# Gates, projections and merge computed with tokens on partitions in a two-layer decoder trunk

## What is computed

```python
xn = rms_norm(x, norm_mix_g[l])
gates = sigmoid(xn @ w_gate[l] + b_gate[l]).reshape(B, S, 4, D)
merged = (gates[:, :, 0] * (ya @ w_proj_a[l]) + gates[:, :, 1] * (yb @ w_proj_b[l])
          + gates[:, :, 2] * (yc @ w_proj_c[l]) + gates[:, :, 3] * (yd @ w_proj_d[l]))
x = x + merged @ w_o[l]
hn = rms_norm(x, norm_ffn_g[l])
x = x + (silu(hn @ w_gate_half) * (hn @ w_up_half)) @ w_ffn_out[l]
```

## Time and profile before

| | us |
|---|---|
| median of 3 runs | 843.73 |
| lowest and highest run | 842.5 and 844.55 |
| the profiled execution, time | 843.07 |
| the profiled execution, span | 841.3 |

### The profile page before, as it was taken

The page is one execution under the profiler, slowest core; times in us unless marked ns, Lnnn a source line. Parts: engine busy times, 40 slices in busy tenths (PEclk is TensorE's granted clock), DMA queues, the critical chain, the costliest instruction groups (busy, mean ns, idle before and its releaser), DMA issues.

```text
span 841.3 us, 15196 instructions
## 1 busy us (share of the span) xinstructions
PE 826.8 (98%) x6199; PEld 783.6 (93%) x6199; DVE 615.8 (73%) x729; ACT 465.9 (55%) x658; POOL 161.1 (19%) x153
## 2 busy tenths in 40 slices
PE   7999999999999999999999999999999999999995
PEld 6999999999989999999999999999999999999995
DVE  5889987776786657665787999767678766566654
ACT  5856787625554555445464567855346454545452
POOL 2814764065000000000000474503300000000000
PEclk9999999999999999999999999999999999999998
DMA  8884544558464554645567464445545456554621
GB/s 261 265 258 138 187 151 154 174 176 237 150 200 145 207 199 155 226 168 200 157 214 230 151 201 152 150 151 165 190 150 198 153 197 207 192 184 165 215 112 50
DMA packets 122070, 152.15 MB, mean 181 GB/s; under 512 B 3824, under 2 KB 109634, under 8 KB 122016
## 3 DMA queue, kind: packets, MB, share of 16 engines
q1 hardware_dynamic: 119392, 148.39, 54.0%
q0 software_dynamic: 1328, 1.81, 0.9%
q10 hardware_dynamic: 1296, 1.20, 0.4%
HBM read 148.23 MB, written 1.05 MB: 177 GB/s over the span
## 4 chain that ended last, share of the span: by engine, by line
PE 93%; DVE 3%; ACT 2%; issue 1%; DMA 1%; ACTq 0%; DVEq 0%
PE bank L875 19%; PE bank L876 19%; PE bank L877 19%; PE bank L941 19%; PE bank L943 10%; PE bank L932 1%; PE bank L934 1%; PE bank L933 1%; DVE w_lo L1274 1%; ACT w_hi L589 1%; PE bank L1025 1%; DMA gain_rows<-in_norm_ffn_g 1%; DVE sq L1305 1%; PE bank L1046 1%; PE bank L921 0%
## 5 line engine op out<-in xcount | busy, mean ns | idle before, releaser
L1274 DVE TENSOR_TENSOR w_lo<-raw,w_hi 128x2048 fp32r<-128x2048 f32 x136 | 318.8, 2347 | 126.8 <-ACT w_hi L589 126.3
L589 ACT ACTIVATE w_hi<-raw 128x2048 fp32r<-128x2048 f32 (+1 forms) x144 | 264.1, 1839 | 146.1 <-PE bank L877 124.2
L941 PE MATMUL bank<-act,w_hi 128*128 128x512 f32 x704 | 246.6, 393 | 0.0
L875 PE MATMUL bank<-act,w_hi 128*128 128x256 f32 x768 | 220.0, 286 | 2.1 <-DVE w_lo L1568 1.0
L876 PE MATMUL bank<-act,w_hi 128*128 128x256 f32 x768 | 217.3, 283 | 0.0
L877 PE MATMUL bank<-act,w_lo 128*128 128x256 f32 x768 | 217.3, 283 | 0.0
L943 PE MATMUL bank<-act,w_lo 128*128 128x256 f32 x704 | 197.1, 280 | 0.0
L941 PEld LDWEIGHTS bank<-act,w_hi 128*128 128x128 f32 x704 | 131.8, 187 | 28.7
L875 PEld LDWEIGHTS bank<-act,w_hi 128*128 128x128 f32 x768 | 147.3, 192 | 4.6 <-issue 2.1
L876 PEld LDWEIGHTS bank<-act,w_hi 128*128 128x128 f32 x768 | 147.4, 192 | 0.1
L877 PEld LDWEIGHTS bank<-act,w_lo 128*128 128x128 f32 x768 | 147.3, 192 | 0.0
(11 more groups left out here) (219 smaller groups left out, 1032.4 us busy)
## 6 DMA issues: line engine op xcount, KB each, us to landing
raw<-in_w_ffn_in SPq DMA_DIRECT2D x44, 1024.0 KB, 5.1
raw<-in_w_gate SPq DMA_DIRECT2D x32, 1024.0 KB, 5.5
raw<-in_w_ffn_out SPq DMA_DIRECT2D x22, 1024.0 KB, 4.9
raw<-in_w_in SPq DMA_DIRECT2D x20, 1024.0 KB, 6.0
raw<-in_w_o SPq DMA_DIRECT2D x8, 1024.0 KB, 5.1
raw<-in_w_proj_b SPq DMA_DIRECT2D x4, 1024.0 KB, 4.9
gates<-qk SPq DMA_DIRECT2D x32, 64.0 KB, 4.7
raw<-in_w_proj_a SPq DMA_DIRECT2D x2, 1024.0 KB, 4.9
```

The lines of the kernel that those rows point to most:

```text
L589: return nc.scalar.activation(o, i, ACT.Copy)
L875: nc.tensor.matmul(o, whi, ahi, start=first, stop=False, skip_group_check=skip)
L941: nc.tensor.matmul(bank[b + f], hi[:, k, fs], act2[:, k, :, :].rearrange("p h s -> p (h s)"), start=(k == 0), stop=False, skip_group_check ...
L1274: V.tensor_tensor(w_lo[slot][:, :], raw[slot][:, :], w_hi[slot][:, :].bitcast(F32), ALU.subtract)\
```

## The change

The 16 gate units of a layer come in pairs. A pair covers 512 weight columns: its first unit holds the first half of the contraction, its second unit the other. Tokens are stationary, 512 weight columns move: 24 matmuls in a unit. A pair fills two banks, one for each half of the tokens. The projections use the same layout (`proj_rows`). The gates' bias now varies along the free axis, so it is loaded from HBM over all partitions (`load_bias`, seven loads in a layer), and DVE multiplies by 1/rms and adds the bias in one instruction (`gate_in`). The merged sum has tokens on partitions, so PE transposes it (`merged_turn`, 8 transposes after unit 30 and 8 after unit 32). The output projection takes its contraction in halves: units 32 and 33 use the first half for channels 0 to 511 and 512 to 1023, units 34 and 35 the second (`unit_wo`, still 48 matmuls 256 wide). Updates of x move accordingly.

```diff
+def pair_of(u):
+    branch, j = gate_of(u)
+    nth = (u - U_GATE) // 2 if u < U_PROJ_A else 6 + j // 2
+    return branch, j // 2, nth, [(u - j % 2 + t) % 4 for t in range(2)]
+BIAS_LOADS = {14: (0, 0), 15: (0, 1), 19: (2, 0), 21: (2, 1), 23: (1, 0), 25: (1, 1), 26: (3, 0)}
...
@@ sync @@
+            def load_bias(l, branch, h):
+                if branch == 3:
+                    buf, n = 2, 2 * 512
+                    sp.wait_ge(s_done, (l + 1) * 2 * HP)
+                else:
+                    buf, n = h, 512
+                    nth = GATE_BRANCH.index(branch)
+                    if nth:
+                        for u in (U_GATE + 4 * (nth - 1) + 2 * h, U_GATE + 4 * (nth - 1) + 2 * h + 1):
+                            sp.wait_ge(bank_free[u % 4], free_at(l, u % 4, f"unit{u}", True))
...
+                sp.dma_start(bias_bufs[buf][:, 0:n], T["b_gate"][l][c0:c0 + n].partition_broadcast(P))\
+                    .then_inc(bias_in[buf], 16)
...
@@ scalar @@
+                elif gate_of(u) and gate_of(u)[1] % 2 == 1:
+                    branch, h, _, bt = pair_of(u)
+                    for t in range(TT):
+                        act.wait_ge(bank_free[bt[t]], free_at(l, bt[t], f"unit{u - 1 + t}", True))
+                        k = branch * KT + 4 * h + 2 * t
+                        nc.scalar.activation(gates[:, k:k + 2, :], gates[:, k:k + 2, :], ACT.Tanh, scale=0.5)\
+                            .then_inc(gate_ready, 1)
+                elif u in (U_GATE_D + 2, U_WO):
+                    for i in (0, 1) if u < U_WO else (2, 3):
+                        act.wait_ge(mt_done, l * 4 + i + 1)
+                        copy(y_hi[:, 2 * i:2 * i + 2, :], low(4 + i)).then_inc(act_hi_ready, 1)
+                elif u in (U_WO + 2, U_WO + 3):
+                    for i in (0, 1) if u == U_WO + 2 else (2, 3):
+                        xg_hi(l, 1, i)
...
-                if U_WO <= u < U_FFN:
-                    square(l, 1, u - U_WO)
+                if u in (U_WO + 2, U_WO + 3):
+                    for i in (0, 1) if u == U_WO + 2 else (2, 3):
+                        square(l, 1, i)
...
-                    urgent = u in (U_WO - 1, U_FFN - 1)
+                    urgent = u > U_GATE_D
...
@@ tensor @@
+            def unit_tokens(slot, half, out_banks, tile=None):
...
+                    for k in range(4):
+                        kk = 4 * half + k
+                        nc.tensor.matmul(o, act_hi[:, kk, ts], hi[:, k, :], start=(kk == 0), stop=False)
+                        nc.tensor.matmul(o, act_hi[:, kk, ts], lo[:, k, :], start=False, stop=False)
+                        last = nc.tensor.matmul(o, act_lo[:, kk, ts], hi[:, k, :], start=False, stop=(kk == KT - 1))
...
+            def merged_turn(l, h):
+                pe.wait_ge(merged_ready, l * 4 + 2 * h + 2)
...
+                            last = nc.tensor.transpose(low(b)[:, f, t * P:(t + 1) * P],
+                                                       merged(2 * h + t)[:, (2 * j + f) * P:(2 * j + f + 1) * P],
+                                                       ident[:, :])
+                    last.then_inc(mt_done, 1)
...
+                    if u == U_GATE_D + 2:
+                        merged_turn(l, 0)
...
+                for j in range(4):
+                    u, (kh, c) = U_WO + j, divmod(j, 2)
                     weights(l, u % RING, u // RING)
...
+                    pe.wait_ge(act_lo_ready, l * 12 + (4 + 2 * kh + 2))
...
+                    unit_wo(u % RING, kh, c)
+                    if j == 0:
+                        merged_turn(l, 1)
...
-                    if i == 3:
-                        norm_stat(l, 1)
                     for f in range(2):
                         last = ffn_half(slot, 0, f, (2 * i, 2 * i + 1))
                         if f == 0 and i == 3:
                             last.then_inc(half_done, 1)
+                            norm_stat(l, 1)
...
@@ vector @@
+                V.scalar_tensor_tensor(gates[:, k:k + 2, :], low(bt[t]), rms_t[:, t:t + 1],
+                                       gate_bias(branch, h).rearrange("p (f s) -> p f s", f=2),
+                                       ALU.mult, ALU.add)\
+                    .then_inc(bank_free[bt[t]], 1)
...
+                if u in (U_GATE_D + 1, U_GATE_D + 3):
...
+                    for t in range(TT):
+                        gate_in(l, u, t)
+                        merge_d(l, 2 * h + t)
...
+                if u == U_WO + 2:
+                    dve.wait_ge(tile_done, l * 10 + 9)
+                    x_update(l, 1, 0)
                     unit_done(l, u)
...
+                    x_update(l, 1, 1)
+                    xg_lo(l, 1, 0)
+                    xg_lo(l, 1, 1)
+                if u == U_WO + 3:
+                    dve.wait_ge(tile_done, l * 10 + 10)
+                    x_update(l, 1, 2)
+                    square_sum(l, 1, 1)
+                    xg_lo(l, 1, 2)
+                    unit_done(l, u)
+                    x_update(l, 1, 3)
+                    square_sum(l, 1, 2)
+                    xg_lo(l, 1, 3)
+                    square_sum(l, 1, 3)
```

More of the change, by code:

```diff
@@ L188, in build @@
         par = sb("par", [P, N_ROWS])
-        half_bg = sb("half_bg", [P, 32])
         half_cn = sb("half_cn", [P, 4])
@@ L282, in build @@
         merged_ready = sem("merged_ready")
+        mt_done = sem("mt_done")
+        tile_done = sem("tile_done")
+        bias_in = [sem(f"bias_in{i}") for i in range(3)]
         madd_done = sem("madd_done")
@@ new lines, in proj_rows @@
+            def proj_rows(slot, b0, k0, first, last_k, done=None, order=range(4), free=None):
+                hi, lo = wide(w_hi[slot]), wide(w_lo[slot])
+                for nth, dp in enumerate(order):
+                    if free is not None:
+                        bank_wait(free[0], b0 + dp, free[1])
+                    h, t = divmod(dp, 2)
+                    ts, cs, o = slice(t * P, t * P + P), slice(512 * h, 512 * h + 512), bank[b0 + dp][:, :]
+                    for k in range(2):
+                        y = y_hi[:, k0 + k, ts]
+                        nc.tensor.matmul(o, y, hi[:, k, cs], start=first and k == 0, stop=False, skip_group_check=True)
+                        nc.tensor.matmul(o, y, lo[:, k, cs], start=False, stop=False, skip_group_check=True)
+                        last = nc.tensor.matmul(o, y_lo[:, k0 + k, ts], hi[:, k, cs], start=False,
+                                                stop=last_k and k == 1, skip_group_check=True)
+                    if done is not None and nth < 3:
+                        last.then_inc(done, 1)
+                last.then_inc(w_used[slot], 1)
@@ L945, in ffn_half, with unit_rows @@
                 return last
-            def unit_rows(slot, b0, hi_in, lo_in, first, last_k, done=None, order=range(4), free=None):
+            def unit_rows(slot, e, last_k, done=None):
                 hi, lo = wide(w_hi[slot]), wide(w_lo[slot])
-                for nth, dp in enumerate(order):
-                    if free is not None:
-                        bank_wait(free[0], b0 + dp, free[1])
+                for dp in range(4):
                     for f in range(2):
@@ L1095, in proj @@
                 first, complete = u != U_PROJ_B + 1, u != U_PROJ_B
-                unit_rows(u % RING, b0, [y_hi[:, k0 + k, :] for k in range(2)], [y_lo[:, k0 + k, :] for k in range(2)],
-                          first, complete, done=pj_done if complete and which != "D" else None,
+                proj_rows(u % RING, b0, k0, first, complete, done=pj_done if complete and which != "D" else None,
                           order=ORDER_A if which == "A" else range(4), free=(l, which) if first else None)
```

183 lines of the change are left out of this document (92 added, 91 removed).

## The result

| | before | after |
|---|---|---|
| median of 8 runs, us | 843.62 | 846.05 |
| lowest and highest | 842.28 to 844.77 | 845.31 to 846.81 |
| the profiled execution: time, span | 843.07, 841.3 | 845.31, 843.6 |

The changed kernel takes 1.003 of the time, 95% interval 1.0019 to 1.0041: **slower by 0.3%**, some 2.4 us. The forecast was 843.7, no change, with the slower side at 0.26; the measured time lies inside its range.

The account below looks back on a forecast made before the run. The prediction took PE, busy for 98% of the span, to bound the kernel. Its terms, -12.2 + 3.5 + 8.4 + 0.3 = 0.0 us, gave 843.1 for the profiled execution and 843.7 as a median, range 839 to 848.

Parts of the forecast that it names:

- What bounds the kernel: Whole kernel: PE, busy for 98% of the span; only its back-to-back instruction time and new waits on it count.
- Part 1: Gate and projection units, 42 in all: 512-wide matmuls take 5.47 us a unit instead of 5.76, 12.2 us less.
- Rivals 2: Gate units: wide matmuls keep less of their advantage and go at 0.232; 8.0 saved, 847.9 us; chance 0.14.
- 4 (no gain from width): Wide units: a 512-wide matmul takes what two narrow ones do, 0.24; nothing saved, 855.9 us; chance 0.02.
- Part 2: Transposes of the merged sum, 4 blocks of 8 at 0.11 us each on PE, without a wait: 3.5 us more.
- Rival 3: Transposes wait for the merged sum as later hand-overs use up the 0.8 margin; 845.7 us and more; chance 0.06.
- Part 3: Entry to the feed-forward block: late x updates make PE wait in unit 36 and before unit 38; 8.4 us more.
- E + 14.1: Entry to the feed-forward block: square sum forecast ready 14.1 us after E, the end of unit 34.
- rival 5: PE's clock falls at the new waits; 4.8 us more, 848.5 us; chance 0.04.
- Part 4: Small terms: PE waits for layer 0's attention probabilities, 0.3 us more, once; bound 0 to 1.
- The sum: Whole kernel: -12.2 + 3.5 + 8.4 + 0.3 = 0.0 us, so no change.
- Rival 1: Feed-forward entry costs half or less, say DVE takes x part 2 before the split; 835.3 to 839.5 us; chance 0.15.

Follow-up runs that it names:

- e2_order: Changed kernel with ACT's and DVE's order behind units 34 and 35 rewritten, the split of unit 37 right behind the first scaled part: 836.96 us.
- e1_fill: Changed kernel with idle matmuls of zeros on PE while it waits before the third (10) and fourth (30) step of unit 36: 843.9 us.
- e7_fill4: Changed kernel with 30 idle matmuls of zeros before the fourth step of unit 36 only: 843.09 us, one run.
- e8_fill3: Changed kernel with 10 idle matmuls of zeros before the third step of unit 36 only: 846.17 us, one run.
- e4_probs: Changed kernel with the normalization of the probabilities ahead of the gates' work in units 11, 14, 17 and 20 on DVE and ACT: 844.41 us, one run.
- e5_both: Changed kernel with e2_order's order and e4_probs' order of the normalization together: 837.03 us.
- e3_narrow: Changed kernel with each 512-wide matmul of the gate units cut into two 256 wide, projections still wide: 854.98 us.

## Why the prediction was right and wrong

- **What bounds the kernel**: right. All that moved the time was PE's pace and PE's waits, in the change and in all eight experiments.
- **Part 1**, 12.2 us less: right, 12.7. It was sized by unit 7 with its slower first matmul; in the steady stream a unit takes 5.44 instead of 5.47. Rivals 2 (a pace of 0.232) and 4 (no gain from width) are out: 0.2267, and cutting the gates' matmuls in two brings 0.29 a unit back. By the 2.5 ns that the Trainium skill gives an isolated warm matmul (TensorE: Matmul & The Clock Gate, Back-to-back issue gap) that cut would have cost an estimated 0.06 a unit. The runs show five times that, so the measurement decides. The same section says that its formula doesn't give the pace of a stream of weight loads and matmuls, which is what runs here; I had left that out.
- **Part 2**, 3.5 us more, no wait: right, 3.6, and doubling them adds 3.5 in the traces. Rival 3 is out.
- **Part 3**, 8.4 us more: the mechanism was right and the term too small. The chain was forecast to end at E + 14.1 and ended at E + 14.15, with waits of 0.85, 2.02 and 0.19 where 0.9, 2.3 and 0.4 were expected, and e2_order took most of it away by order alone. The 4.2 a layer is also what e1_fill and e7_fill4 show with the clock held up: 16.89 - 12.60 = 4.29. But the changed kernel measured 5.06, over the bound of 4.8, and the 0.77 between is the clock. The step that failed is the sentence "no wait here passes 2.3 us, with full work between", which set **rival 5** at 0.04 and left the clock out of this term: the wait of 2.0 us was enough. Rival 5's price of 4.8 us in all was too high for the changed kernel (1.5 in its profile, 2.1 between its median and e1_fill's), as the time at the lower level was 3.4 us a layer, and part of it would have been spent waiting for DVE. For the longer falls it isn't far off: one of 6.8 us cost 2.2 in a layer of e8_fill3 and 1.9 in one of e4_probs (18.82 against 16.90). I had read a share of busy time at the kernel's end and carried over its size, but no row of before showed PE idle for 2 us in the middle of full work, and an unknown like this has to widen the range of the term it stands behind.
- **Part 4**, 0.3 us more for the probabilities: too small, 1.5 in the profiled execution. I costed one wait, at unit 15, from one execution's DVE and ACT times; there are two, the other at unit 12, and they are larger where unit 7's load lands later. How much of it the median carries is open: e5_both, without them, is no faster than e2_order.
- **The sum**: 0.0 forecast. Of the profiled +2.24, the clock makes +1.5 (0.77 a layer), the probabilities +1.2, parts 2 and 3 without the clock +0.3, and part 1 and the start give 0.8 back. So the forecast missed the slowdown of 2.4 us, and gave that side 0.26 only. That e1_fill, with the clock held up, takes 843.9, next to the forecast's 843.7, is in part luck: the probabilities' 1.2 too much stands against 0.8 too little from part 1 and the start. And that 846.05 lies inside the range of 839 to 848 is no merit of the account, since the range left rival 5 out.
- **Rival 1**, that DVE takes x part 2 ahead of the split, isn't what the change does. e2_order comes to the same price another way, with the split ahead of x part 2 but earlier: 836.96, between this rival's 835.3 at no cost and 839.5 at half.

## What to carry to other kernels

A change that makes the bounding engine's work shorter can lose it all in one hand-over, where an order written for the old production order makes that engine wait; follow the helper engines' written order there, and rewrite it with the change: here that was worth 9 us, some 2 of them the clock's. Where a stall of some 2 us on TensorE stays, count the clock's fall behind it as a possible cost of its own, and look for it in windows of a few us: in the page's slices of 21 us a fall of 3.4 us doesn't show, and one of 6.8 only as an 8. Then either remove the stall or fill it with idle matmuls. A wait of a few tenths that hangs on a load's landing differs from one execution to the next, and one profile doesn't size it.

## What the runs showed of the hardware that was not expected

- TensorE's granted clock fell to 0.50 behind a wait of 2.0 us in 6 of 8 layers, each time when the engine was already at work again. Three falls began 1.3 to 1.9 us after the end of the wait and lasted 3.4 us (the changed kernel, both layers; e3_narrow, layer 1). Three began 0.3 to 0.8 us after it and lasted 6.8 us (layer 0 of e3_narrow, e4_probs and e8_fill3). A wait of 0.85 us alone (e7_fill4, two layers), or 2 us filled with 30 matmuls of zeros (e1_fill and e7_fill4, four layers), brought no fall.
- At the lower level a pair of matmuls 512 and 256 wide takes 0.64 us, 768 columns at 1.2 GHz: the 13 ns that each matmul costs over its columns at the upper level isn't there. At the upper level the pair takes 0.35.
- The Trainium skill (TensorE: Matmul & The Clock Gate, A second HAM failure mode: psum-queue depth-cycling) tells of a kernel whose frequent short idle times between groups of matmuls made the clock fall and rise again. The traces here show the same falling and rising with another pattern: a single idle time of 2.0 us in the middle of full work.
